# Expert layer of a two-layer diffusion step: fixed experts' weights requested first, ring slots handed out by which is left first, the next layer's weights held behind the read-back, and six output sums begun ahead of the last down product

## The chip, the cores and the metric

One core of one Trainium2 chip. The metric is device time in microseconds (us) of one execution. Engines are called as the profile calls them: PE (TensorE, matrix products), DVE (VectorE), ACT (ScalarE), POOL (GpSimd) and SP (SyncE, which here issues weight transfers). "DMA" is a transfer between device memory (DRAM) and the on-chip memory.

## The reference, cut to what matters

Two layers (`DEPTH = 2`) run over 384 tokens (128 context, 256 latent) of width 1024. The first half of a layer is attention, convolution and an output projection. The second half is a mixture of experts, and the change lies there:

```python
aff = sigmoid(t @ w_router)                  # 16 experts in 4 groups of 4
g_idx = argmax(sum of the best two of each group)
e_idx = the best two experts in that group   # top 2 per token
gates = their affinities, normalised to sum 1
hid = silu(t @ w_gate[e]) * (t @ w_up[e])    # 1024 -> 512
y = sum over the 2 experts of gates * (hid @ w_down[e])   # 512 -> 1024
x = x + gate2 * y
```

## The kernel before

All weights pass through a ring of 1 MB slots: six in `ring`, and in the expert part of a layer eight more in `extra_ring`, whose memory the rest of the layer uses. SP issues the loads in one fixed list, `RING_ORDER`. Ahead of each load it waits until the slot's earlier content has been used (`left`). It issues in order, so a load that must wait holds back all behind it.

An expert has six loads (`PER_EXPERT`): 0 and 1 are its gate matrix, 2 and 3 its up matrix, 4 and 5 its down matrix. The 16 experts form 11 units (`UNITS`): six of one expert (128 rows) and five of two experts with 64 rows each. Places 0 and 1 always hold experts 0 and 1 (`FIXED = 2`), so their loads need no routing result. Which expert stands in places 2 to 15 is decided by how crowded it is; SP reads that from `order_i` after DVE has set `order_known`. PE takes the units one after another: gate product of unit u+1, transposed hidden rows of u, up product of u+1, turned token rows of u+2, then `down(u, 0)` and `down(u, 1)`, the two halves of the down product of u. `STREAM` lists the loads in that order of use.

The outputs of units 0 to 8 are scattered by POOL to `y_rows` in DRAM and, when the last scatter has landed, read back in three transfers of 1 MB, one for each tile of 128 tokens, into `parts[0]`, `parts[1]` (both in `late`) and `parts[2]` (in `y`). ACT scales a part (`scale_part`, L1839 as called from there), DVE weighs it and adds the second half (`weigh_part`, L2552). The outputs of the last two units (9 and 10) stay on the chip: ACT and DVE split them into `y_split` (`y_high` L1848, `y_rest` L2560). For each tile t and half q of the columns a sum "A" is then collected in a PSUM bank: `add_most` is one product of the identity with the weighed part (L1420) and two products with unit 9's rows (L1430); `add_rows(t, q, LAST - 1)` adds two products with unit 10's rows. DVE multiplies each finished sum by the layer's gate and adds it to `x` (`add_last`, L2650 and L2653). In the first layer the next layer's norm follows on the same engine, in the second the output stores.

Both DVE and ACT run their lists in order. On DVE the end of a layer reads: `y_rest` of unit 9, `weigh_part` of tiles 0, 1, 2, `y_rest` of unit 10, then the sums.

Of the kernel before, what the change touches and what calls it, by code (L numbers as in the profile page):

```python
# [117 lines left out]
STREAM += unit_stream(NU - 1, 4, 6)  # L118
UNIT_OF = {k: u for u in range(NU) for k in UNITS[u]}
# [4 lines left out]
def ring_order():  # L124

    order = [(n, 2 * k + i) for n, k in FIRST_PAIRS for i in range(2)]
    for n in range(DEPTH):
        for i, js in enumerate(STAGES):
            order += [(n, S_IN + j) for j in js]
            order += [(m, 2 * k + h) for m, k in pairs_after(n, "proj", i) for h in range(2)]  # L130
            if i == S_UP_AFTER:
                order.append((n, S_UP))
        order += [(m, 2 * k + i) for m, k in pairs_after(n, "heads") for i in range(2)]
        order.append((n, S_UP + 1))
        for g in range(len(GROUPS) + 2):
            order += [(m, 2 * k + i) for m, k in pairs_after(n, "turn", g) for i in range(2)]
        order += [(n, S_OUT + j) for j in range(OUT_SLOTS)]
        order += [(n, S_EXP + e * PER_EXPERT + i) for e, i in STREAM]
# [194 lines left out]
def slots_by_turn():  # L333

    at, taken, base = [], [0] * (RING + EXTRA), 0
    before = []
    last = [None] * (RING + EXTRA)
    j = 0
    for q, (n, s) in enumerate(RING_ORDER):
        if s < S_EXP:  # L340
            r, base, j = base % RING, base + 1, 0
        else:
            if j == 0:
                cycle = [(base + i) % RING for i in range(RING)] + [RING + i for i in range(EXTRA)]
            r, j = cycle[j % len(cycle)], j + 1
# [4 lines left out]
        if s >= S_EXP and j == NE * PER_EXPERT:  # L350
            base = cycle[0]
# [14 lines left out]
def build(nc, wring, x_in, vec, rows, ckv_cache, kr_cache, nak_cache, nav_cache, cond, w_router,  # L366
          b_router, rope, shape_consts, na_bias, row_ids, no_token,
          y_prompt, y_sample, new_ckv, new_krope, new_nak, new_nav, h_rows, y_rows, tables, mod_dram):
    with ExitStack() as ctx:
# [332 lines left out]
        def _(sp):  # L702
            sp.dma_start(condT, cond).then_inc(cond_loaded, 16)
            q, expert = 0, {}
            for n in range(DEPTH):
                l = Layer(n)

# [246 lines left out]
        def _(pe):  # L954
# [180 lines left out]
            for n in range(DEPTH):  # L1135
# [300 lines left out]
                list_rows(0)  # L1436
                gate_or_up(0, "G", 0, sems["gate_half"])
# [3 lines left out]
                for u in range(NU):  # L1441
# [13 lines left out]
                    if u == NU - 2:  # L1455
                        turn_hidden(NU - 1)
                        for i in range(LAST):
                            turn_hot(i)
                    down(u, 1)

                with pe.If(extra > 0):
# [4 lines left out]
                    for i in range(LAST):  # L1466
                        pe.wait_ge(*once_read(l, (f"turned{i}",)))
                    with pe.Fori(0, extra) as w:
                        with pe.Fori(0, NE) as e:
# [25 lines left out]
                            pe.wait_ge(more_y_made[n], w * NE + (e + 1))  # L1495

                halves = [(t, q) for t in range(TILES) for q in range(2)]

                for t, q in halves[:3]:
                    add_most(t, q)  # L1500
                for t, q in halves[:3]:
                    add_rows(t, q, LAST - 1)
                for t, q in halves[3:]:
                    add_most(t, q)
# [1282 lines left out]
```

## Time and profile before

| what | value |
|---|---|
| median of 3 runs | 1071.9 us (1068.68 to 1073.7) |
| the profiled execution's own time | 1071.57 us |
| its span, first to last instruction | 1069.8 us |
| PE busy | 1006.7 us, 94% of the span |
| mean granted clock of PE | 0.97 of full |
| expert part of the first layer | from about 294 to 558 us |
| expert part of the second layer | from about 786 to 1052 us |

Times in the rows are microseconds from the start of the span. A timeline row gives start, duration, engine, source line, operation, output and inputs and the count of instructions merged in it; in brackets the idle time ahead of it and what ended it. One matrix product stands as two instructions in the trace. PEclk is the clock that PE was granted, 1.00 being 2.4 GHz and 0.50 being 1.2 GHz.

### The profile page before, as it was taken

How to read it: one execution, taken by the hardware profiler on the slowest of the kernel's cores; microseconds unless marked ns; L12 is line 12 of the kernel's file. 1: busy time of each engine (PE TensorE's matmuls, PEld its weight loads, DVE VectorE, ACT ScalarE, POOL GpSimd, SP SyncE). 2: the span in 40 equal slices, each digit the busy share in tenths (PEclk: the TensorE clock that was granted, in tenths of full speed). 3: DMA queues.
4: the chain of work that ended last, by engine and by line, in shares of the span. 5: the costliest groups of instructions: out<-in, count | busy, mean ns of one | idle time of the engine just before them, and what ended most of it. 6: DMA issues, size and time to landing. Idle time of an engine off the chain costs nothing.

```text
span 1069.8 us, 12824 instructions
## 1 busy us (share of the span) xinstructions
PE 1006.7 (94%) x4770; PEld 593.0 (55%) x4770; DVE 418.2 (39%) x861; ACT 290.9 (27%) x629; POOL 143.7 (13%) x192
## 2 busy tenths in 40 slices
PE   5899898999999999999979999889999999999975
PEld 1686556678854434444338976668874444343422
DVE  1348824586451010000136679767462100101014
ACT  2333265572111011010035337754210111101110
POOL 2200411201110000100101015201020110001000
PEclk9899989999899999999999999978999999999998
DMA  9778396864899999999981225104499999999971
GB/s 376 292 277 342 137 360 274 337 254 195 312 368 362 421 392 422 421 420 422 420 349 57 106 79 163 43 9 197 161 383 391 377 399 423 421 420 422 421 300 59
DMA packets 51376, 320.52 MB, mean 300 GB/s; under 512 B 8718, under 2 KB 8830, under 8 KB 16368
## 3 DMA queue, kind: packets, MB, share of 16 engines
q1 hardware_dynamic: 38448, 276.59, 63.9%
q0 software_dynamic: 12864, 43.08, 10.6%
q8 instruction: 40, 0.66, 0.2%
q14 instruction: 24, 0.20, 0.0%
HBM read 307.08 MB, written 21.25 MB: 307 GB/s over the span
## 4 chain that ended last, share of the span: by engine, by line
PE 76%; DVE 9%; DMA 8%; ACT 3%; issue 2%; POOL 1%; SPq 0%; DVEq 0%; POOLq 0%; ACTq 0%
PE bank L1372 26%; PE bank L1399 12%; PE bank L978 6%; PE bank L1249 5%; PE bank L996 4%; PE bank L961 3%; PE bank L1108 3%; DMA extra_ring<-wring_dram 3%; DMA y<-y_rows 2%; PE bank L1073 2%; PE bank L1039 2%; DMA ring<-wring_dram 2%; PE bank L968 2%; PE bank L1356 2%; PE bank L1285 1%
## 5 line engine op out<-in xcount | busy, mean ns | idle before, releaser
L1372 PE MATMUL bank<-ring,hgT 128*64 128x512 f32 (+1 forms) x512 | 156.4, 594 | 2.1 <-DMA ring<-wring_dram 1.6
L1372 PE MATMUL bank<-extra_ring,hgT 128*64 128x512 f32 (+1 forms) x512 | 155.9, 594 | 0.0
L1399 PE MATMUL bank<-extra_ring,hidT 128*64 128x512 f32 (+1 forms) x352 | 111.8, 624 | 9.7 <-DMA extra_ring<-wring_dram 9.7
L2533 DVE TENSOR_TENSOR sg<-bank,sg 128x512 f32<-128x512 f32 x22 | 15.2, 691 | 252.2 <-PE bank L1372 252.2
L1372 PEld LDWEIGHTS bank<-ring,hgT 128*64 128x64 f32 (+1 forms) x512 | 58.5, 157 | 87.5 <-issue 87.5
L1372 PEld LDWEIGHTS bank<-extra_ring,hgT 128*64 128x64 f32 (+1 forms) x512 | 58.3, 157 | 86.6 <-issue 86.5
L1399 PEld LDWEIGHTS bank<-extra_ring,hidT 128*64 128x64 f32 (+1 forms) x352 | 40.9, 163 | 71.4 <-issue 71.4
L2278 DVE SCALAR_TENSOR_TENSOR conv_acc<-conv_in,vecs,conv_acc 128x399 f32<-128x399 f32 x120 | 70.9, 632 | 2.1
L1108 PE MATMUL bank<-ring,cond_p 128*32 128x512 f32 x384 | 53.3, 675 | 17.0 <-DMA ring<-wring_dram 16.2
L978 PE MATMUL bank<-ring,hT 128*128 128x256 f32 x288 | 66.5, 392 | 2.6 <-DVE hT L1924 2.6
L889 POOL DMA_INDIRECT y_rows<-y,y_at x18 | 18.2, 1011 | 368.2 <-DVE y L2542 348.0
L762 POOL TENSOR_TENSOR rstd<-ms,half 128x28 f32<-128x28 f32 (+3 forms) x10 | 32.7, 3272 | 231.2 <-DVE ms L1900 231.2
L978 PEld LDWEIGHTS bank<-ring,hT 128*128 128x128 f32 x288 | 56.2, 197 | 11.6 <-DVE hT L1924 2.8
L1788 ACT COPY hgT<-bank 128x512 f32<-128x512 f32 x24 | 14.0, 585 | 167.3 <-PE bank L1356 140.4
L2542 DVE COPY y<-bank 128x512 f32<-128x512 f32 x18 | 12.4, 692 | 113.4 <-PE bank L1399 113.4
L1797 ACT ACTIVATE sg<-bank 128x512 f32<-128x512 f32 x22 | 13.1, 597 | 153.0 <-PE bank L1372 153.0
L1399 PE MATMUL bank<-ring,hidT 128*64 128x512 f32 (+1 forms) x160 | 49.6, 595 | 0.0
L1039 PE MATMUL bank<-kT,qT 96*128 96x128 f32 (+3 forms) x144 | 44.1, 441 | 0.2 <-ACT probsT L1648 0.2
L2018 DVE TENSOR_REDUCE rowmax<-bank 128x1 f32<-128x384 f32 (+1 forms) x56 | 24.8, 442 | 49.6 <-PE bank L1039 48.0
L1811 ACT COPY y<-bank 128x512 f32<-128x512 f32 x18 | 10.5, 585 | 107.6 <-PE bank L1399 107.6
L1249 PE MATMUL bank<-out_hi,mixT_hi 128*128 128x512 f32 x96 | 38.8, 404 | 1.1 <-DVE mixT_lo L2346 0.7
L1640 ACT ACTIVATE probs<-bank,negmax,qscale 128x384 f32<-128x384 f32 (+1 forms) x48 | 28.2, 594 | 34.9 <-DVE negmax L2021 34.8
(315 smaller groups left out, 1532.7 us busy)
## 6 DMA issues: line engine op xcount, KB each, us to landing
ring<-wring_dram SPq DMA_DIRECT2D x150, 1024.0 KB, 12.8
extra_ring<-wring_dram SPq DMA_DIRECT2D x108, 1024.0 KB, 17.8
y_rows<-hg POOLq DMA_DIRECT2D x6, 1024.0 KB, 6.2
kT<-mod_dram POOLq DMA_DIRECT2D x4, 1024.0 KB, 9.8
late<-y_rows POOLq DMA_DIRECT2D x4, 1024.0 KB, 15.5
ring<-wring_dram SPq DMA_DIRECT2D x4, 832.0 KB, 19.5
h_rows<-h_tok POOLq DMA_DIRECT2D x6, 512.0 KB, 6.2
ring<-wring_dram SPq DMA_DIRECT2D x4, 640.0 KB, 11.1
```

The costliest lines, as they stand in the source:

```text
L762: pool.tensor_tensor(rstd[:, 0:n], ms[:, 0:n], half[:].broadcast_to([P, n]), ALU.pow) \
L961: mm = pe.transpose(b[0:d, i * P:(i + 1) * P], part, iden[:])
L978: mm = pe.matmul(b[:, 0:n], hT[:, c, t * P:(t + 1) * P], w[:, c, :], start=(c == 0), stop=(c == KC - 1))
L996: mm = pe.matmul(b[:, 0:n], a, w, start=((c, k) == (0, 0)), stop=((c, k) == (KC - 1, 2)))
L1039: mm = pe.matmul(b[:, 0:hi - lo], qT[0:d, s, h, t * P:(t + 1) * P], kT[0:d, s, h, lo:hi], start=True, stop=True)
L1108: mm = pe.matmul(bank[b][32 * i:32 * (i + 1), :], cond_p[:, s % 2 * 4 + i, at:at + 32], w[:, i, :], start=first, stop=last)
L1249: mm = pe.matmul(b[:, :], a, w, start=((c, k) == (0, 0)), stop=((c, k) == (KC - 1, 2)))
L1372: mm = pe.matmul(b[lo:hi, :], hgT[:, 4 * i + c, lo:hi], in_ring(l, expert_slot(place, s + i))[:, c * 512:(c + 1) * 512], start=((i, c) == ...
L1399: mm = pe.matmul(b[m][lo:hi, :], hidT[:, u % 2, 2 * i + c, lo:hi], in_ring(l, expert_slot(place, 4 + i))[:, at:at + 512], start=((i, c) == ...
L1640: act.activation(out, b[:, 0:hi - lo], ACT.Exp, bias=negmax[:, g, t:t + 1], scale=qscale[:, p, 4 * t + h:4 * t + h + 1] if p < 2 else 1.0, ...
L2018: dve.tensor_reduce(rowmax[:, t:t + 1], b[:, 0:n], AX, ALU.max).then_inc(sems["dve_step"], 1)
L2278: ins = dve.scalar_tensor_tensor(conv_acc[:, c, :], conv_in[:, c, k:k + C_OUT], tap, conv_acc[:, c, :], ALU.mult, ALU.add)
```

## The change

Four edits.

1. `LOADS` replaces `STREAM` as the list in which expert weights are requested: all twelve loads of places 0 and 1 come first, then the others in the order of use as before. Two loads, the down matrix of place 1, so move ahead of the first load that needs `order_known`.
2. `slots_by_turn` no longer hands out slots in a fixed cycle. It takes the slot whose content is used up first (`left_at`).
3. At the start of the second layer's loads SP waits until all three parts of the first layer's read-back have landed (`parts_loaded`).
4. `add_most` for all six sums stands between `down(10, 0)` and `down(10, 1)`; after the last down product only the six `add_rows` for unit 10 are left. (In the branch for overfull experts, which isn't taken with these inputs, the sums are closed and begun again.)

```diff
@@ plan of the loads
+LOADS = [(k, i) for k in range(FIXED) for i in range(PER_EXPERT)] + [(k, i) for k, i in STREAM if k >= FIXED]
+USED_AT = {ki: a for a, ki in enumerate(STREAM)}
...
-        order += [(n, S_EXP + e * PER_EXPERT + i) for e, i in STREAM]
+        order += [(n, S_EXP + e * PER_EXPERT + i) for e, i in LOADS]
@@ slots_by_turn
-            if j == 0:
+            if left_at is None:
                 cycle = [(base + i) % RING for i in range(RING)] + [RING + i for i in range(EXTRA)]
-            r, j = cycle[j % len(cycle)], j + 1
+                left_at = {r: i - len(cycle) for i, r in enumerate(cycle)}
+            r = min(left_at, key=left_at.get)
+            left_at[r] = USED_AT[divmod(s - S_EXP, PER_EXPERT)]
...
-        if s >= S_EXP and j == NE * PER_EXPERT:
-            base = cycle[0]
+        if s >= S_EXP and (q + 1 == len(RING_ORDER) or RING_ORDER[q + 1][0] != n):
+            base = min(range(RING), key=left_at.get)
@@ SP, at the head of a layer
+                if n:
+                    for t in range(TILES):
+                        sp.wait_ge(parts_loaded[t], 16 * n)
@@ PE, the loop over units
+                    if u == NU - 1:
+                        for t, q in halves:
+                            add_most(t, q)
                     down(u, 1)
...
-                for t, q in halves[:3]:
-                    add_most(t, q)
-                for t, q in halves[:3]:
-                    add_rows(t, q, LAST - 1)
-                for t, q in halves[3:]:
-                    add_most(t, q)
+                for t, q in halves:
                     add_rows(t, q, LAST - 1)
```

The order of SP's instructions where the first layer's expert loads begin, in the kernel before. `bank_full...`, `x_mid`, `h_added` and `h_made` are the events that free the eight extra slots; L723 reads a routing result, L725 is a load that needs one, L719 a load that needs none.

```order
L719 DMA extra_ring<-wring_dram 128x2048 [waits bank_full3] x4
L723 TENSOR_LOAD order_i [waits order_known,bank_full4]
L723 ISA x2
L725 ISA
L725 DMA extra_ring<-wring_dram 128x2048
L723 TENSOR_LOAD order_i [waits order_known,x_mid,bank_full6]
L723 ISA x2
L725 ISA
L725 DMA extra_ring<-wring_dram 128x2048
L725 ISA [waits h_added,h_made]
```

The same place in the changed kernel (its L729, L733 and L735 are the L719, L723 and L725 of before):

```order
L729 DMA extra_ring<-wring_dram 128x2048 [waits bank_full3] x4
L729 DMA extra_ring<-wring_dram 128x2048 [waits bank_full4]
L729 DMA extra_ring<-wring_dram 128x2048 [waits x_mid,bank_full6]
L733 TENSOR_LOAD order_i [waits order_known,h_added,h_made]
L733 ISA x2
L735 ISA
L735 DMA extra_ring<-wring_dram 128x2048
L733 TENSOR_LOAD order_i [waits order_known,h_made]
L733 ISA x2
L735 ISA
L735 DMA extra_ring<-wring_dram 128x2048
L735 ISA [waits gate_half]
```

Six loads instead of four stand ahead of the wait for the routing result, and behind it two slots instead of four are free without a wait for PE. From the twenty-first expert load of a layer (the first load of place 4) on, each load stands at the same place in the list and waits for the same earlier expert load to be used up as before; only the slot's number differs.

SP's first loads of the second layer, before and then in the changed kernel:

```order
L719 DMA ring<-wring_dram 128x2048 [waits bank_full0] x2
L719 DMA ring<-wring_dram 128x1664 [waits up_half] x2
L719 DMA ring<-wring_dram 128x2048 [waits bank_full1]
L719 DMA ring<-wring_dram 128x1280 [waits bank_full1]
L719 DMA ring<-wring_dram 128x2048 [waits bank_full0]
```

```order
L729 DMA ring<-wring_dram 128x2048 [waits parts_loaded2,gate_half,parts_loaded1,parts_loaded0]
L729 DMA ring<-wring_dram 128x2048 [waits gate_half]
L729 DMA ring<-wring_dram 128x1664 [waits bank_full0] x2
L729 DMA ring<-wring_dram 128x2048 [waits down_half]
L729 DMA ring<-wring_dram 128x1280 [waits down_half]
```

The first of these six loads gains the three waits for the read-back, and all behind it stand behind that.

PE's instructions at the end of the first layer, before, from the first sum on. Ahead of them stand both halves of unit 10's down product (L1399) and the branch that isn't taken:

```order
L1420 MATMUL bank<-late,shapes 128x512
L1430 MATMUL bank<-y_split_81,turned_hot_70 128x512 x2
L1420 MATMUL bank<-late,shapes 128x512
L1430 MATMUL bank<-y_split_81,turned_hot_70 128x512 x2
L1420 MATMUL bank<-late,shapes 128x512
L1430 MATMUL bank<-y_split_81,turned_hot_70 128x512 x2
L1430 MATMUL bank<-y_split_83,turned_hot_89 128x512 x6
L1420 MATMUL bank<-late,shapes 128x512
L1430 MATMUL bank<-y_split_81,turned_hot_70 128x512 x2
L1430 MATMUL bank<-y_split_83,turned_hot_89 128x512 x2
```

In the changed kernel (L1409, L1430 and L1440 are the L1399, L1420 and L1430 of before), from inside the six sums to the last half of the down product, L1409; the first half and the first identity product stand just ahead:

```order
L1440 MATMUL bank<-y_split_81,turned_hot_70 128x512 x2
L1430 MATMUL bank<-late,shapes 128x512
L1440 MATMUL bank<-y_split_81,turned_hot_70 128x512 x2
L1430 MATMUL bank<-late,shapes 128x512
L1440 MATMUL bank<-y_split_81,turned_hot_70 128x512 x2
L1430 MATMUL bank<-late,shapes 128x512
L1440 MATMUL bank<-y_split_81,turned_hot_70 128x512 x2
L1430 MATMUL bank<-y,shapes 128x512
L1440 MATMUL bank<-y_split_81,turned_hot_70 128x512 x2
L1430 MATMUL bank<-y,shapes 128x512
L1440 MATMUL bank<-y_split_81,turned_hot_70 128x512 x2
L1409 MATMUL bank<-extra_ring,hidT 64x512 x8
```

The last half of the down product has moved behind the sums that read `y`, the third part of the read-back.

## Rows read from the trace of the kernel before

**Rows 1.** Head of the page: span, busy time of PE.

```profile
span 1069.8 us, 12824 instructions
PE 1006.7 (94%) x4770; PEld 593.0 (55%) x4770; DVE 418.2 (39%) x861; ACT 290.9 (27%) x629; POOL 143.7 (13%) x192
```

**Rows 2.** Waits of PE: us in total, times, longest.

```profile
PE bank L1399 <- DMA extra_ring<-wring_dram: 9.7, 4, 4.1
```

**Rows 3.** The chain that ended last, end of the first layer: start, us, what.

```profile
528.23 25.87 DMA y<-y_rows
...
557.40 0.72 PE bank L1430 x2
...
558.26 0.70 DVE gated_sum L2650
...
570.08 3.69 PE bank L978 x16
```

**Rows 4.** Timeline, end of the first layer.

```profile
523.42 11.45 SPq L719 DMA_DIRECT2D ring<-wring_dram  x6
...
539.94 3.65 PE L1399 MATMUL bank<-extra_ring,hidT 128*64 128x512 f32 x16 [1.06 <-DMA extra_ring<-wring_dram]
...
546.38 1.15 ACT L1839 ACTIVATE late<-late,gate 128x1024 f32<-128x1024 f32 x1 [5.74 <-DMA late<-y_rows]
547.56 1.28 DVE L2552 SCALAR_TENSOR_TENSOR late<-late,gate 128x1024 f32<-128x1024 f32 x1 [5.60 <-ACT late L1839]
...
547.64 5.11 PE L1399 MATMUL bank<-extra_ring,hidT 128*64 128x512 f32 x16 [4.05 <-DMA extra_ring<-wring_dram]
```

**Rows 5.** Timeline, end of the second layer.

```profile
1034.77 5.35 PE L1399 MATMUL bank<-extra_ring,hidT 128*64 128x512 f32 x16 [2.30 <-DMA extra_ring<-wring_dram]
...
1042.38 5.21 PE L1399 MATMUL bank<-extra_ring,hidT 128*64 128x512 f32 x16 [2.25 <-DMA extra_ring<-wring_dram]
...
1043.20 1.15 ACT L1839 ACTIVATE y<-y,gate 128x1024 f32<-128x1024 f32 x1 [3.59 <-DMA y<-y_rows]
...
1044.38 1.28 DVE L2552 SCALAR_TENSOR_TENSOR y<-y,gate 128x1024 f32<-128x1024 f32 x1 [3.45 <-ACT y L1839]
...
1047.55 1.55 DVE L2560 SCALAR_TENSOR_TENSOR y_split<-bank,gate_slot,y_split 128x512 fp32r<-128x512 f32 x2 [1.89 <-ACT y_split L1848]
...
1048.94 1.02 PE L1420 MATMUL bank<-late,shapes 128*128 128x512 f32 x2
...
1050.26 1.02 PE L1420 MATMUL bank<-late,shapes 128*128 128x512 f32 x2
...
1052.25 0.69 DVE L2650 TENSOR_TENSOR gated_sum<-bank,kT 128x512 f32<-128x512 f32 x1 [3.15 <-PE bank L1430]
```

**Rows 6.** The chain that ended last, end of the second layer.

```profile
1009.04 33.20 DMA extra_ring<-wring_dram
```

**Rows 7.** Stretches: us, busy of engines, PEclk, DMA share, GB/s.

```profile
295.00:300.00 5.00, 5.00 (x47) 4.74 (x46) 4.72 (x14) 1.24 (x3) 0.00 (x0) 1.00 0.53 187
...
335.00:340.00 5.00, 5.00 (x18) 1.89 (x18) 0.69 (x1) 0.58 (x1) 0.24 (x1) 1.00 0.80 254
...
530.00:535.00 5.00, 5.00 (x20) 2.21 (x17) 0.69 (x1) 0.00 (x0) 0.00 (x0) 1.00 1.01 416
```

**Rows 8.** Expert loads issued 334 to 340 us, from issue to landing.

```profile
DMA to landing us min/median/max: 4.7/4.8/5.0
```

**Rows 9.** The same, 826 to 832 us, second layer.

```profile
DMA to landing us min/median/max: 4.9/5.2/5.5
```

**Rows 10.** Expert loads issued 996 to 1012 us, from issue to landing.

```profile
DMA to landing us min/median/max: 25.9/27.7/33.2
```

**Rows 11.** Waits of SP: us in total, times, longest.

```profile
SPq L722 <- DVE order_i L2172: 29.6, 2, 15.1
```

**Rows 12.** DMA queues from 530 to 556 us (q1 SP's, q0 POOL's).

```profile
q1 hardware_dynamic: 1089, 7.35, 67.9%
q0 software_dynamic: 816, 3.15, 30.4%
```

**Rows 13.** Stretches at the end of the second layer: us, PE busy, PEclk, DMA, GB/s.

```profile
1036.00:1038.00 2.00, 2.00 (x8) 0.50 0.43 178
1040.00:1042.00 2.00, 0.12 (x2) 1.00 0.12 51
```

More of the change, by code:

```diff
@@ L337, in slots_by_turn @@
     last = [None] * (RING + EXTRA)
-    j = 0
+    left_at = None
     for q, (n, s) in enumerate(RING_ORDER):
         if s < S_EXP:
-            r, base, j = base % RING, base + 1, 0
+            r, base, left_at = base % RING, base + 1, None
         else:
-            if j == 0:
+            if left_at is None:
                 cycle = [(base + i) % RING for i in range(RING)] + [RING + i for i in range(EXTRA)]
-            r, j = cycle[j % len(cycle)], j + 1
+                left_at = {r: i - len(cycle) for i, r in enumerate(cycle)}
+            r = min(left_at, key=left_at.get)
+            left_at[r] = USED_AT[divmod(s - S_EXP, PER_EXPERT)]
         at.append((r, taken[r]))
@@ L1436, in _ @@
                 list_rows(0)
+                halves = [(t, q) for t in range(TILES) for q in range(2)]
                 gate_or_up(0, "G", 0, sems["gate_half"])
@@ L1467, in _ @@
                         pe.wait_ge(*once_read(l, (f"turned{i}",)))
+                    for t, q in halves:
+                        pe.matmul(bank[bank_no(l, (f"A{t}{q}",))][:, :], iden[:], parts[t][:, 0, 512 * q:512 * (q + 1)], start=False, stop=True)
                     with pe.Fori(0, extra) as w:
@@ L1495, in _ @@
                             pe.wait_ge(more_y_made[n], w * NE + (e + 1))
-                halves = [(t, q) for t in range(TILES) for q in range(2)]
-                for t, q in halves[:3]:
-                    add_most(t, q)
-                for t, q in halves[:3]:
-                    add_rows(t, q, LAST - 1)
-                for t, q in halves[3:]:
-                    add_most(t, q)
+                    for t, q in halves:
+                        add_most(t, q)
+                for t, q in halves:
                     add_rows(t, q, LAST - 1)
```

## The prediction

> **What bounds the kernel now.** I began with the page's head: PE is busy for 1006.7 of 1069.8 us [rows 1], so time is won or lost only where PE waits, runs at a lower clock, or has nothing left but a chain on other engines. The list of PE's waits comes next. Its largest in the expert part is the down product's: four waits on loads, 9.7 us in all [rows 2], two at the end of each layer. The chain that ended last and the timeline show what surrounds them. In the first layer the two halves of unit 10's down product start at 539.94 and 547.64, the second after 4.05 us of waiting and at a reduced pace, 5.11 us instead of 3.65 [rows 4]. Then the chain leaves PE: it runs through the third part of the read-back (`parts[2]`, tile 2's, "part 3" from here on), which lands at 528.23 + 25.87 = 554.10, and DVE takes up the first finished sum at 558.26; layer 2's first projection follows at 570.08 [rows 3]. In the second layer the halves start at 1034.77 and 1042.38, with waits of 2.30 and 2.25 us, and DVE starts on the sums at 1052.25 [rows 5]. There the chain goes back through the last expert load, 33.20 us from issue to landing [rows 6]. From DVE's first sum on, both ends run at DVE's pace in the kernel before and after, so **the start of DVE's first sum is the number to predict in each layer**.
>
> The stretches tell what the transfers do. Around 295 to 300 us, ahead of the routing result, they run at 187 GB/s; at 335 to 340 again only at 254; at 530 to 535 at 416 with every DMA engine busy [rows 7]. So they are late at the end and idle at the start of an expert part.
>
> **Loads of the fixed experts first, and the slots: 0 us.** SP waits for `order_i` twice, at most 15.1 us [rows 11]; two loads more, 2 MB, now go out ahead of it. At 416 GB/s a load of 1 MB takes 2.5 us, so the two fill 5.0 us of the gap; that is the most this edit could give in one layer. I take nothing, because of what comes behind. The loads issued between 334 and 340 us, the 23rd and 24th of the layer, land 4.7 to 5.0 us after issue [rows 8], in the second layer 4.9 to 5.5 [rows 9]; those issued at the end take 25.9 to 33.2 [rows 10]. A load that lands in 4.7 us has no queue ahead of it: at that moment the transfers wait for PE to free a slot. From the 21st load on each load waits for the same content to be used up as before. So whatever is gained ahead is handed back there, and the queue that makes the last loads late is built up only afterwards. The work that hides the edit is PE's own products up to there. Slots "by which is left first" only keep, for the new list, the order of use that the old cycle gave the old list. A loss from loads that now come later (the second gate loads of places 2 and 3, about 4 us) I exclude: at 335 to 340 the transfers have caught up and PE is busy throughout [rows 7].
>
> **Holding back the next layer's weights: part 3 lands about 5 us earlier, but only in the first layer.** Before, SP issues six loads for layer 2 at 523.42 to 534.87 [rows 4], behind the last expert loads, and from about 547.5 they share the DMA engines with part 3. The second layer, which has no such loads, shows part 3 without them: it lands at 1043.20 [rows 5], 0.96 us after the last expert load (1009.04 + 33.20 = 1042.24 [rows 6]). Put at the first layer's last load, 547.5, that gives 548.5; part 2's landing at 546.38 [rows 4] is the lower bound, since the parts follow one another, and 554.10, no gain, the upper one. I take 549. Parts 1 and 2 don't move; they landed while the expert loads were still in front. The loads held back start at about 549 too. With 4.7 us to land for the first [rows 8], it is there at 554 and all six by 554 + 5 x 2.5 = 566.5, ahead of the 570.08 at which the first is read [rows 3]: 16 us of cover for that one, so 0 us. If part 3 were as late as before, 11 us would remain.
>
> One rule bears on this. From 530 to 556 us SP's queue moved 1089 packets and 7.35 MB, POOL's 816 packets and 3.15 MB [rows 12]. The Trainium skill (DMA: Bandwidth & Descriptors, Queues, rings and completion order) says that each DMA engine takes turns between its queues packet by packet. By that rule the two queues are level in packets and POOL's, with the smaller ones, gets less than half of the bytes; the trace agrees. Had the turns been level in bytes, the three parts would have been in by about 528.2 + 6 x 2.5 = 543, and holding back would give nothing; the trace has 554.10, and the sum goes by that.
>
> **The six sums ahead of the last half of the down product: a gain behind it, a larger loss ahead of it.** From one `add_most` to the next are 1050.26 - 1048.94 = 1.32 us [rows 5], so the six take 7.9 us, 2.64 us for a tile. Behind the last half DVE today waits until 1052.25, that is 1052.25 - (1042.38 + 5.21) = 4.66 us. With the sums begun ahead, what remains is `y_rest` and one `add_rows`: the first half of DVE's pair at 1047.55 ends 0.7 us later at 1048.25, two instructions on PE take 0.72 [rows 3] with 0.14 of hand-over on either side, together 1.66 us behind the end of the product. That gains 3.0 us. But PE executes in order, and the last half now stands behind the two sums that read part 3. Part 3 must land, be scaled (1.15) and weighed (1.28): 1043.20 to 1045.66 [rows 5]. Behind that come 0.14, two sums of 2.64, the product of 3.65 and the 1.66, which makes 8.1 us.
>
> *Second layer.* The first half ends at 1040.12. Tile 0 runs to 1042.9, tile 1 to 1045.5, tile 2 from 1045.8 (weighed at 1045.66) to 1048.45; the last half then takes 3.65, because PE no longer stops for 2.25 us ahead of it, and ends at 1052.1; DVE starts at 1053.75 instead of 1052.25: **+1.5 us**. Were part 3 there at once, PE alone would give 1040.12 + 0.14 + 7.92 + 3.65 + 1.66 = 1053.5, +1.25: the lower bound. If the clock still falls once, as it did, 1.56 more: +3.1.
>
> *First layer.* The first half ends at 543.6, tile 0's sums at 546.4. Part 2 is weighed at 547.56 + 1.28 = 548.84 [rows 4], so PE waits 2.6 us, which it doesn't do there before. Both waits of 2.3 us in the second layer were followed by about 3.4 us at the lower of the two clocks (0.50 in 1036 to 1038 [rows 13]) and cost 1.70 and 1.56 (5.35 and 5.21 for a product of 3.65 [rows 4, 5]); I charge 1.6. Tile 1 is then done at 553.2, tile 2 (part 3 weighed at 551.5) at 555.9, the product at 559.5, and DVE starts at 561.2 instead of 558.26: **+2.9 us**. Without the fall of the clock, and part 3 in time, 551.6, 554.3, 557.9, 559.6: +1.3. With part 3 as late as 554.10 the end would be 554.10 + 2.46 + 8.1 = 564.7: +6.4; this value is far from the rows of the second layer, and I leave it out of the range. PE also has nothing to do for some 2.7 us ahead of layer 2's first transposes, where the moved sums filled the time; if the clock falls there too, up to 1.7. I take 0, since ACT and DVE set the pace there.
>
> Sum: 0 + 2.9 + 1.5 = 4.4 us on the profiled 1071.57, which lies 0.3 below the median: **1076.0 us**, 0.4% slower. About 0.5%, 5.4 us, is what a measurement of this kernel can tell from no change, so the likeliest verdict is "same".
>
> **Rivals.**
> - *The clock falls at more places* (layer 2's start 1.7, the second layer's last half 1.6): 1076.0 + 3.3 = 1079.3, slower by 0.7%. For it: both waits in [rows 5] had a fall behind them. Against it: PE's new gap in the second layer is 0.2 us. The Trainium skill (TensorE: Matmul & The Clock Gate, The HAM clock gate) says that the low clock is the resting state and that only activity releases it; by that rule this rival holds wherever the moved sums leave PE without work.
> - *The lead of the loads lasts to the end: faster.* Place: the queue at the 23rd load. If the 5.0 us survived there, loads and parts would land 5 us earlier at both ends. The second layer's DVE start would be 1043.20 - 5.0 + 2.46 + 8.1 = 1048.75, -3.5; the first's, bound by PE without waits, about 543.6 - 1.06 + 0.14 + 7.92 + 3.65 + 1.66 = 555.9, -2.4; together -5.9: 1065.7. It decides for "faster" only if nearly all of the 5.0 us survive; the 4.7 us of [rows 8] and 4.9 of [rows 9] speak against that.
> - *The sums cost less than they seem and the change is worth nothing*: no fall of the clock, part 3 in by 548. That is +1.3 + 1.25 = 2.6, 1074.2; with the runs' own scatter it reads as no change.
>
> **How the numbers follow.** Forecast and its neighbourhood (1075 to 1077.3) 0.40; no fall of the clock (1071 to 1075) 0.25; more falls, or part 3 later (above 1077.3) 0.29; lead survives 0.06. The range for 8 in 10 reaches from 1071.5 (the third rival less the 0.25% by which the runs scatter) to 1079.5 (the first rival). Slower by over 0.5% gets the 0.29, faster the 0.06, within 0.5% the remaining 0.65.
>
> **What would show it.** Loads: SP's `order_i` wait remains, loads around 335 us again land in about 4.8 us, and PE reaches 539.9 and 1034.8 (plus the first layer's shift) as before. Holding back: layer 2's six loads are issued at about 549, part 3 lands there too, and no PE wait for `ring` appears at layer 2's first projection. Sums: a PE wait of about 2.6 us for `part_weighed` between the halves in the first layer, with PEclk 0.50 behind it; the last half starts at about 556 and, counted from the same point, 6 us later than before in the second layer; DVE's first sums at about 561 and 1053.75 + 2.9 = 1056.7. I am wrong if the 23rd load's latency is no measure of the queue, if part 3 lands several us ahead of 549, or if the last half doesn't wait for it.

## The result

The changed kernel takes 1079.85 us (median of 20 runs, 1074.2 to 1091.0), the kernel before 1073.05 beside it: ratio **1.0067, 95% interval 1.0041 to 1.0094**, some 7 us slower. The forecast was 1076.0 with 1079.5 as its upper end; the time fell just beyond it, where the first rival (the clock falls at more places, 1079.3) had put it.

The span of the profiled execution is 1081.9 us, that of a second one, shown further down as e11, 1069.7. Single spans are no measure here, so the stages are read from points inside them. The page's span, which was 1069.8 before [rows 1], then PE's waits against [rows 2]:

```profile
span 1081.9 us, 12826 instructions
```

```profile
PE bank L971 <- DVE xn L1927: 5.2, 2, 2.6
PE bank L1409 <- DMA ring<-wring_dram: 3.2, 2, 2.3
...
PE bank L1430 <- DVE y L2564: 2.3, 2, 1.9
PE bank L1430 <- DVE late L2564: 2.2, 1, 2.2
```

The 9.7 us of waits for loads have become 3.2; the 4.05-us wait ahead of the last half [rows 4] is gone. In their place stand waits for the weighed parts (L1430) and, at layer 2's start, for the norm (L971). Lines are 10 higher than before on PE: L1409 is the down product, L1430 the identity product and L1440 the products with a unit's rows. The timeline of the first layer's end, to be held against [rows 4]:

```profile
542.31 3.65 PE L1409 MATMUL bank<-ring,hidT 128*64 128x512 f32 x16 [0.87 <-DMA ring<-wring_dram]
...
550.97 1.10 PE L1430 MATMUL bank<-late,shapes 128*128 128x512 f32 x2 [2.17 <-DVE late L2564]
...
551.61 1.15 ACT L1851 ACTIVATE y<-y,gate 128x1024 f32<-128x1024 f32 x1 [2.10 <-DMA y<-y_rows]
551.74 3.42 SPq L729 DMA_DIRECT2D ring<-wring_dram  x6
...
554.22 1.10 PE L1430 MATMUL bank<-y,shapes 128*128 128x512 f32 x2 [0.37 <-DVE y L2564]
...
557.03 3.65 PE L1409 MATMUL bank<-extra_ring,hidT 128*64 128x512 f32 x16
...
562.55 0.69 DVE L2662 TENSOR_TENSOR gated_sum<-bank,kT 128x512 f32<-128x512 f32 x1 [0.27 <-DVE a L2235]
...
569.29 1.09 PE L971 MATMUL bank<-shapes,xn 128*128 128x128 f32 x8 [2.59 <-DVE xn L1927]
572.97 1.97 PE L971 MATMUL bank<-shapes,xn 128*128 128x128 f32 x8 [2.59 <-DVE xn L1927]
574.73 5.09 PE L988 MATMUL bank<-ring,hT 128*128 128x256 f32 x16
```

As foretold, PE waits for part 2 (2.17 us), the held-back loads go out when part 3 is there (551.74), the last half runs at full pace and DVE's first sum follows it closely. The wait of 0.37 us for part 3 was not foretold, nor was what follows: layer 2's first projection takes 5.09 us, behind two gaps of 2.59 us on PE. The kernel before had one gap of 1.44 us there and the full pace:

```profile
568.68 1.09 PE L961 MATMUL bank<-shapes,xn 128*128 128x128 f32 x8 [1.44 <-DVE xn L1915]
570.08 3.69 PE L978 MATMUL bank<-ring,hT 128*128 128x256 f32 x16 [0.31 <-DVE hT L1924]
```

The same view at the second layer's end, against [rows 5]:

```profile
1043.66 3.65 PE L1409 MATMUL bank<-ring,hidT 128*64 128x512 f32 x16 [2.31 <-DMA ring<-wring_dram]
...
1052.09 1.15 ACT L1851 ACTIVATE y<-y,gate 128x1024 f32<-128x1024 f32 x1 [4.08 <-DMA y<-y_rows]
...
1054.70 1.19 PE L1430 MATMUL bank<-y,shapes 128*128 128x512 f32 x2 [1.90 <-DVE y L2564]
...
1056.54 1.91 PE L1430 MATMUL bank<-y,shapes 128*128 128x512 f32 x2
...
1059.15 3.65 PE L1409 MATMUL bank<-extra_ring,hidT 128*64 128x512 f32 x16
...
1064.41 0.69 DVE L2662 TENSOR_TENSOR gated_sum<-bank,kT 128x512 f32<-128x512 f32 x1
```

PE waits 1.90 us for part 3, and an identity product of 1.02 us takes 1.91. The granted clock (the number ahead of the DMA share and the GB/s) in four stretches, with PE's busy time behind the length:

```profile
551.00:553.00 2.00, 2.00 (x7) 1.18 (x7) 0.21 (x1) 1.15 (x1) 0.00 (x0) 1.00 0.23 41
...
571.00:574.00 3.00, 1.03 (x5) 1.03 (x6) 2.93 (x7) 2.15 (x8) 0.43 (x1) 0.50 0.00 0
...
1053.00:1055.00 2.00, 0.30 (x1) 0.30 (x2) 1.28 (x1) 0.24 (x1) 0.00 (x0) 1.00 0.00 0
1056.00:1058.00 2.00, 2.00 (x5) 1.03 (x4) 0.00 (x0) 0.00 (x0) 0.00 (x0) 0.50 0.00 0
```

So the clock fell at layer 2's start and behind part 3 in the second layer, not behind the wait for part 2.

**Where the 7 us are.** From the first half of the last down product to DVE's first sum, split at the last half; starts and durations are those of the rows:

| | first half to last half | last half | its end to DVE's first sum | together |
|---|---|---|---|---|
| first layer before | 7.70 | 5.11 | 5.51 | 18.32 |
| first layer after | 14.72 | 3.65 | 1.87 | 20.24 |
| second layer before | 7.61 | 5.21 | 4.66 | 17.48 |
| second layer after | 15.49 | 3.65 | 1.61 | 20.75 |

The two layers' ends are +1.9 and +3.3. From DVE's first sum to the end of the first 16 projection products it was 570.08 + 3.69 - 558.26 = 15.51 [rows 3] and is 574.73 + 5.09 - 562.55 = 17.27: +1.8. Together 7.0, as timed. That they agree so closely is in part luck: from layer 2's 17th projection product to its last down product PE's work is the same in all the kernels below, and it took from 457.8 us (e11) to 468.8 (e4) in single executions. The stages leave that out.

### The profile page after: what moved, and what is told of

It is laid out like the page before. It is cut to its first block, busy times and chain, and to the rows that moved or that the text cites. A ratio compares the mean times of both kernels' runs of the same rounds, so it can differ in the third digit from the quotient of the medians.

```text
span 1081.9 us, 12826 instructions
## 1 busy us (share of the span) xinstructions
PE 1012.1 (94%) x4770; PEld 600.0 (55%) x4770; DVE 418.1 (39%) x861; ACT 291.8 (27%) x629; POOL 143.7 (13%) x192
## 3 DMA queue, kind: packets, MB, share of 16 engines
q0 software_dynamic: 12864, 43.08, 10.5%
## 4 chain that ended last, share of the span: by engine, by line
PE 77%; DVE 8%; DMA 8%; ACT 3%; issue 2%; POOL 1%; SPq 0%; DVEq 0%; POOLq 0%; ACTq 0%
PE bank L1382 26%; PE bank L1409 12%; PE bank L988 6%; PE bank L1259 6%; PE bank L1006 4%; PE bank L971 4%; DMA y<-y_rows 4%; PE bank L1118 3%; PE bank L1083 2%; PE bank L1049 2%; DMA ring<-wring_dram 2%; PE bank L978 2%; PE bank L1366 2%; DMA y_rows<-y,y_at 2%; PE bank L1295 1%
## 5 line engine op out<-in xcount | busy, mean ns | idle before, releaser
L1382 PE MATMUL bank<-extra_ring,hgT 128*64 128x512 f32 (+1 forms) x576 | 177.6, 594 | 2.1 <-DMA extra_ring<-wring_dram 1.6
L1382 PE MATMUL bank<-ring,hgT 128*64 128x512 f32 (+1 forms) x448 | 135.1, 594 | 0.0
L1382 PEld LDWEIGHTS bank<-extra_ring,hgT 128*64 128x64 f32 (+1 forms) x576 | 66.9, 158 | 101.4 <-issue 101.3
L1382 PEld LDWEIGHTS bank<-ring,hgT 128*64 128x64 f32 (+1 forms) x448 | 50.0, 156 | 72.7 <-issue 72.7
L1409 PE MATMUL bank<-extra_ring,hidT 128*64 128x512 f32 (+1 forms) x288 | 86.0, 595 | 0.0
L1409 PE MATMUL bank<-ring,hidT 128*64 128x512 f32 (+1 forms) x224 | 71.3, 595 | 3.2 <-DMA ring<-wring_dram 3.2
L1409 PEld LDWEIGHTS bank<-extra_ring,hidT 128*64 128x64 f32 (+1 forms) x288 | 30.9, 155 | 46.3 <-issue 46.3
L1809 ACT ACTIVATE sg<-bank 128x512 f32<-128x512 f32 x22 | 13.1, 597 | 153.0 <-PE bank L1382 153.0
L1409 PEld LDWEIGHTS bank<-ring,hidT 128*64 128x64 f32 (+1 forms) x224 | 26.8, 160 | 40.0 <-issue 40.0
L1823 ACT COPY y<-bank 128x512 f32<-128x512 f32 x18 | 10.5, 585 | 107.6 <-PE bank L1409 107.6
## 6 DMA issues: line engine op xcount, KB each, us to landing
extra_ring<-wring_dram SPq DMA_DIRECT2D x108, 1024.0 KB, 17.7
late<-y_rows POOLq DMA_DIRECT2D x4, 1024.0 KB, 15.3
```

The lines of the kernel that those rows point to most:

```text
L1382: mm = pe.matmul(b[lo:hi, :], hgT[:, 4 * i + c, lo:hi], in_ring(l, expert_slot(place, s + i))[:, c * 512:(c + 1) * 512], start=((i, c) == ...
L1409: mm = pe.matmul(b[m][lo:hi, :], hidT[:, u % 2, 2 * i + c, lo:hi], in_ring(l, expert_slot(place, 4 + i))[:, at:at + 512], start=((i, c) == ...
```

## The experiments

Theory S: PE works in order, so sums ahead of the last half cost their own time and the wait for their part, and PE's gaps let the clock fall. Its rivals vary with the runs. In all of them A and C are the time from the first half of the last down product to DVE's first sum in the first and second layer, B that from the first layer's first sum to PE's 17th projection product of layer 2, each taken from the timeline of one profiled execution. "Stages" is the change of A + B + C against the kernel before, "timed" the ratio's excess times 1073 us. Single entries scatter: among the four kernels without sums ahead (before, e1, e5, e6) A is 17.5 to 19.4 and C 15.9 to 18.5. "Stages" and "timed" differ by up to 4.3 us.

| kernel | sums ahead | held back | A | B | C | stages | ratio (95% interval) | timed |
|---|---|---|---|---|---|---|---|---|
| before | 0 | no | 18.3 | 16.2 | 17.5 | | | |
| changed | 6 | yes | 20.2 | 18.0 | 20.8 | +7.0 | 1.0067 (1.0041 to 1.0094) | +7.2 |
| e1 | 0 | yes | 17.5 | 17.9 | 17.2 | +0.6 | 1.0023 (0.9987 to 1.0059) | +2.5 |
| e2 | 6 | no | 25.2 | 17.7 | 19.5 | +10.5 | 1.0124 (1.0081 to 1.0167) | +13.3 |
| e3 | 2 | yes | 13.4 | 16.4 | 13.4 | -8.8 | 0.9955 (0.9919 to 0.9990) | -4.8 |
| e4 | 6 | yes | 20.6 | 16.2 | 20.2 | +5.0 | 1.0086 (1.0049 to 1.0122) | +9.2 |
| e5 | 0 | yes | 17.5 | 16.2 | 15.9 | -2.4 | 1.0018 (0.9988 to 1.0048) | +1.9 |
| e6 | 0 | no | 19.4 | 16.2 | 18.5 | +2.2 | 1.0006 (0.9975 to 1.0037) | +0.6 |
| e7 | 2 | yes | 13.0 | 16.4 | 13.2 | -9.4 | 0.9930 (0.9896 to 0.9964) | -7.5 |
| e8 | 4 | yes | 16.1 | 17.7 | 16.0 | -2.2 | 0.9962 (0.9933 to 0.9991) | -4.1 |
| e9 | 6 | yes | 17.2 | 18.5 | 17.0 | +0.7 | 0.9995 (0.9963 to 1.0028) | -0.5 |
| e10 | 2 | no | 17.9 | 17.7 | 13.1 | -3.3 | 0.9964 (0.9933 to 0.9996) | -3.9 |
| e11 | 6 | yes | 20.6 | 17.9 | 19.8 | +6.4 | one execution, 1071.72 us | |
| e12 | 2 | no | 15.3 | 17.4 | 14.8 | -4.5 | 0.9958 (0.9929 to 0.9988) | -4.5 |

**e1: the changed kernel with the sums behind the product again.**

```diff
-                    if u == NU - 1:
-                        for t, q in halves:
-                            add_most(t, q)
                     down(u, 1)
```

> The changed kernel with the six sums back behind the last down product (edits 1 to 3 stay). Theory S (the moved sums cost all of it: the last half of the down product waits for part 3, and the clock falls in the gaps that the move leaves): part 3 no longer stands ahead of anything, DVE's first sum in the first layer comes about 0.9 us earlier than in the kernel before, second layer as before: about 1072, -0.1%. Theory H (holding back the weights costs, at layer 2's start): it stays near 1080, +0.6%. Theory L (the loads' new order or the slots cost): it stays near 1080, +0.6%.

The median is 1075.31, between S's 1072 and the 1080 of H and L. The interval holds no change and excludes the changed kernel's 0.67%, but the two intervals overlap (up to 1.0059, from 1.0041), so this run alone does not settle how much of the loss is the sums'; e2, e3 and e9 do. B is 17.9 here too: the clock fell behind a gap of 1.53 us.

**e2: the kernel before with the sums alone**, the last two pieces of the change's diff:

```diff
+                    if u == NU - 1:
+                        for t, q in halves:
+                            add_most(t, q)
                     down(u, 1)
```

> The kernel before with the six sums ahead of the last half of the down product, nothing else. Theory S: part 3 lands in the first layer as late as before, about 9 us behind the last expert load's predecessor (554 instead of 549), so DVE's first sum there comes 6.4 us later, plus up to 1.8 of lower clock at layer 2's start; second layer +3.3 as in the changed kernel: about +10 to +12 us, +0.9 to +1.1%, slower than the changed kernel. Theories H and L: no loss, 1073.

Slower by 1.2%, as S has it. Of the first layer's end, the scaling of part 3 and PE's wait for it:

```profile
553.21 1.15 ACT L1841 ACTIVATE y<-y,gate 128x1024 f32<-128x1024 f32 x1 [6.01 <-DMA y<-y_rows]
...
555.82 2.05 PE L1420 MATMUL bank<-y,shapes 128*128 128x512 f32 x2 [4.28 <-DVE y L2554]
```

Part 3 is there 1.6 us later than in the changed kernel, although the first half started earlier (541.27 against 542.31); PE waits 4.28 us instead of 0.37, and the low clock follows (2.05 us for the two products at L1420). With six sums ahead, A is 5.0 us shorter in the changed kernel, which has the hold-back and the new order of the loads as well; e6 and e7 put the order at nothing measurable, so the 5.0 are put down to the hold-back (e10 against e7: 4.9).

**e3 and e8: two and four sums ahead.** In e3, and in e8 with 4 for 2:

```diff
-                        for t, q in halves:
+                        for t, q in halves[:2]:
                             add_most(t, q)
...
-                for t, q in halves:
+                for t, q in halves[:2]:
+                    add_rows(t, q, LAST - 1)
+                for t, q in halves[2:]:
+                    add_most(t, q)
                     add_rows(t, q, LAST - 1)
```

> The changed kernel with only the two sums of tile 0 ahead of the last half of the down product, the other four behind it. Theory S: these two wait for part 1 alone, which is weighed before the first half ends, and fill PE's wait for the last load (2.3 us in the second layer, 4.0 in the first), so no gap, no fall of the clock: second layer DVE's first sum 4 us earlier than before, first layer 5 us earlier: about 1064, -0.9%. Theory H or L (the sums are not the cause): 1076 to 1080.

> The changed kernel with tile 0's and tile 1's four sums ahead, tile 2's behind the last half. Theory S (each pair ahead costs its 2.64 us and the wait for its part): the last half starts at about 553.6 in the first layer and 1052.5 in the second, as in the changed kernel without tile 2's sums; DVE's first sum is 1.9 us earlier than in the kernel before in the first layer, 3.3 in the second; together 3.5 to 4 us later than with two ahead: ratio 0.998 to 1.000, 1071 to 1073. Rival C (only the wait for part 3 costs, and with it the lower clock; PE's time for the sums is free): as with two ahead, 0.9955, about 1069.

Both are faster than the kernel before, by some 0.4%, with intervals that end below 1. A and C grow with each pair, 13.4, 16.1, 20.2 and 13.4, 16.0, 20.8. In the stages two ahead gains what S gave; the time, 1069.09, is 5 us above S's 1064, and S's 0.9% lies just outside the interval. Four ahead is 1070.68: as S's 1071 to 1073 and C's 1069 lie so close, the times don't tell them apart, but the stages do (C had two and four alike). That two ahead is faster than four is so shown by the stages of one execution each, not by the times.

**e9: no wait for a later part.** The sums of tiles 1 and 2 are started from part 1 instead of their own part, so their results, and what the second layer works on, are of other data:

```diff
-                    pe.wait_ge(sems["part_weighed"], nth(l, "part_weighed", t + 1))
-                    pe.matmul(..., iden[:], parts[t][:, 0, 512 * q:512 * (q + 1)], start=True, stop=False)
+                    pe.wait_ge(sems["part_weighed"], nth(l, "part_weighed", 1))
+                    pe.matmul(..., iden[:], parts[0][:, 0, 512 * q:512 * (q + 1)], start=True, stop=False)
```

> The changed kernel with all six sums started from part 1 instead of each tile's own part (the second and third tile's sums are of other data), so that PE between the halves of the last down product waits for no later part. Theory S (the loss is PE's waits for parts 2 and 3 ahead of the last half and the lower clock behind them; PE's own 7.9 us for the sums are paid by the 3.0 us behind and the load waits they fill): from the start of the first half to DVE's first sum 17.0 to 17.5 us in both layers, 1.3 and 0.3 less than in the kernel before, layer 2's start still 1.7 longer: ratio 1.000, 1073 to 1074. Rival O (PE's order alone costs it, whatever the parts do): 20 us in both layers as in the changed kernel, ratio 1.006, 1080.

Theory S holds, rival O falls: A 17.2, C 17.0, ratio 0.9995. In the first layer PE runs through from half to half, 11.71 us instead of 14.72:

```profile
538.48 3.65 PE L1409 MATMUL bank<-ring,hidT 128*64 128x512 f32 x16 [1.91 <-DMA ring<-wring_dram]
...
550.19 3.65 PE L1409 MATMUL bank<-extra_ring,hidT 128*64 128x512 f32 x16
```

Layer 2's start keeps its two gaps and takes 18.5 us. The interval (up to 1.0028) lies below the changed kernel's (from 1.0041). The six sums' own time is thus about paid by what they save behind the product; the loss is the waits for parts 2 and 3 and the clock.

**e11: the changed kernel once more.**

> The changed kernel once more, for the scatter of its stages. Theory S: from the first half to DVE's first sum again 20.2 us in the first layer, 20.7 in the second if the clock falls in PE's wait for part 3 there and 19.0 to 19.5 if not; layer 2's start again 18.0; the attention part anywhere from 210 to 220. Rival V (the 1.8 us at layer 2's start and in the second layer are chance): one of the two is gone, 16.2 or 19.

Both held in part: the second layer's end, then layer 2's start.

```profile
1032.30 3.65 PE L1409 MATMUL bank<-ring,hidT 128*64 128x512 f32 x16 [1.51 <-DMA ring<-wring_dram]
...
1044.07 1.10 PE L1430 MATMUL bank<-y,shapes 128*128 128x512 f32 x2 [0.84 <-DVE y L2564]
...
1046.88 3.65 PE L1409 MATMUL bank<-extra_ring,hidT 128*64 128x512 f32 x16
...
563.33 1.09 PE L971 MATMUL bank<-shapes,xn 128*128 128x128 f32 x8 [2.60 <-DVE xn L1927]
567.01 1.97 PE L971 MATMUL bank<-shapes,xn 128*128 128x128 f32 x8 [2.59 <-DVE xn L1927]
568.77 5.01 PE L988 MATMUL bank<-ring,hT 128*128 128x256 f32 x16
```

Layer 2's start is the same, so its loss is not chance. In the second layer the last half follows tile 2's first sum after 2.81 us, not 4.45: no fall behind a wait of 0.84. That fall differs between executions. The 1071.72 us of this execution lie below all 20 of the changed kernel in the result (1074.2 to 1091.0). Against the first profile, the first layer's last down product starts 6.4 us earlier (535.95) and the stretch between B and C is 5.3 us shorter, while A + B + C differ by only 0.6.

**e4: PE kept busy.** The changed kernel with idle identity products in its gaps:

```diff
+                            if (n, t, q) == (0, 1, 0):
+                                keep_busy(l, ("A10",), 8)
+                            if (n, t, q) == (1, 2, 0):
+                                keep_busy(l, ("A20",), 7)
...
-                    keep_busy(l, ("n1", 0, 0), IDLE_FIRST)
+                    keep_busy(l, ("n1", 0, 0), IDLE_FIRST + 10)
...
+                    keep_busy(l, ("n1", 1, 0), 10)
```

> The changed kernel with idle products of the identity in PE's gaps: 8 ahead of tile 1's sums in the first layer, 7 ahead of tile 2's in the second, 10 more ahead of each of layer 2's first two groups of transposes. They add no result. Theory S with the clock as half of the loss: PEclk stays 1.00 from 540 to 580 and from 1040 to 1065 us, layer 2's first projection and the second layer's last half run at full pace, 1.8 us each: about 3.5 us less than the changed kernel, 1076, +0.3%. If the waits alone make the loss and the clock doesn't matter: as the changed kernel, 1080.

A miss: 1081.92, no better than the changed kernel. Yet at layer 2's start it did what it was for:

```profile
566.20 1.09 PE L971 MATMUL bank<-shapes,xn 128*128 128x128 f32 x8 [0.38 <-DVE xn L1932]
...
569.88 1.09 PE L971 MATMUL bank<-shapes,xn 128*128 128x128 f32 x8 [0.36 <-DVE xn L1932]
571.28 3.69 PE L988 MATMUL bank<-ring,hT 128*128 128x256 f32 x16 [0.31 <-DVE hT L1941]
```

Without the gap the fall is gone, and B is 16.2: the gap causes the 1.8 us. In the second layer C changed little, for the fall came at another place. Tile 2's sums, behind the idle products, kept their pace, but this time the first half ran at the low clock, behind a wait of 2.34 us for its load (in the changed kernel it took 3.65 behind 2.31):

```profile
1044.46 5.35 PE L1410 MATMUL bank<-ring,hidT 128*64 128x512 f32 x16 [2.34 <-DMA ring<-wring_dram]
...
1056.68 1.02 PE L1431 MATMUL bank<-y,shapes 128*128 128x512 f32 x2
```

Layer 2's attention, whose instructions are the same, ran at a lower clock in this execution. The stretch from 590 to 770 us, first in the changed kernel, then in e4:

```profile
590.00:770.00 180.00, 171.42 (x888) 139.08 (x888) 131.16 (x248) 89.81 (x209) 35.18 (x37) 0.93 0.26 96
```

```profile
590.00:770.00 180.00, 174.80 (x860) 140.08 (x859) 128.08 (x246) 87.92 (x207) 35.16 (x37) 0.88 0.26 92
```

e9, without idle products, has 0.88 there too and is no slower in the timing. Whether e4's gain is always lost there, or in this execution only, stays open.

**e5 and e6: the other edits alone** on the kernel before. First the diff of e5, then of e6 (with `slots_by_turn` as in the change):

```diff
+                if n:
+                    for t in range(TILES):
+                        sp.wait_ge(parts_loaded[t], 16 * n)
```

```diff
-        order += [(n, S_EXP + e * PER_EXPERT + i) for e, i in STREAM]
+        order += [(n, S_EXP + e * PER_EXPERT + i) for e, i in LOADS]
```

> The kernel before with the hold-back alone. Theory S (the sums cause the loss, the hold-back is harmless): part 3 lands about 5 us earlier in the first layer, DVE's first sum there about 0.9 us earlier, nothing in the second layer: ratio 0.999, about 1072.5. Rival H (the 2 to 4 us that the two kernels with the hold-back lacked against the sum of their stages come from it): 1.002 to 1.004, 1075 to 1078, with layer 2's first projection later against DVE's first sum than the 16.2 us of the kernel before.

> The kernel before with the fixed experts' loads first and the slots by which is left first, nothing else. Theory S: the lead is handed back at the 23rd load, ratio 1.000, 1073. Rival L (this order costs something at the ends of the expert parts): the first half of unit 10's down product starts 1 to 2 us later in a layer, ratio 1.002 to 1.004, 1075 to 1077. Rival E (the lead lasts): down products 2 to 5 us earlier, ratio 0.995.

Neither differs from the kernel before by what this can tell. e5's time, 1075.58, would fit rival H (1075 to 1078) as well; against H speaks B, 16.2 as before, and in e6 it is 16.2 too. Two stretches of the changed kernel show the lead and how it is handed back. From 295 to 300 us the transfers run at 430 GB/s instead of 187, and they slacken (254 at 335 to 340 in [rows 7]) some 5 us sooner, at 330 to 335:

```profile
295.00:300.00 5.00, 5.00 (x47) 5.00 (x46) 4.69 (x17) 0.58 (x1) 0.00 (x0) 1.00 1.02 430
...
330.00:335.00 5.00, 5.00 (x19) 2.57 (x18) 1.39 (x2) 0.58 (x1) 0.00 (x0) 1.00 0.65 242
```

**e7, e10 and e12: what two sums ahead need.** e7 is e3 without the new order of the loads, e10 is e7 without the hold-back, and e12 is e10 with

```diff
-                for t in range(TILES):
+                for t in range(TILES - 1):
                     scale_part(t)
                 y_high(1)
+                scale_part(TILES - 1)
```

and the same on DVE (`weigh_part`, `y_rest`).

> The kernel before with the hold-back and tile 0's two sums ahead, the order of the loads as it was. Theory S (the order of the loads is worth nothing): same as the kernel that has it and two sums ahead, 0.9955, about 1069. Rival L (the order costs 2 to 4 us): 0.992 to 0.9935, 1065 to 1066.

> The kernel before with tile 0's two sums ahead of the last half and nothing else: loads and next layer's weights as before. Theory S (two sums fill PE's wait for the last load and shorten what is behind; the hold-back matters only to a sum that waits for part 3 ahead of the product): like the kernel that holds the weights back as well, ratio 0.993 to 0.996, 1067 to 1070. Rival P (part 3, landing at 554 in the first layer, holds up tile 2's sums behind the product): 2 to 3 us longer than that, ratio 0.997 to 0.999.

> The kernel before with tile 0's two sums ahead and, on ACT and DVE, the last place's y_high(1) and y_rest(1) ahead of the scaling and weighing of part 3; loads and next layer's weights as before. Theory Q (in the first layer DVE's first sum waits for part 3 only because y_rest(1) stands behind its weighing, so the hold-back buys what this order buys): from the start of the last half to DVE's first sum 5.5 us in the first layer instead of 10.2, without the hold-back; ratio 0.992 to 0.994, 1065 to 1067, like two sums ahead with the hold-back. Rival T (tile 2's sums need part 3 soon enough that nothing is won): the first sum comes earlier, but layer 2's first projection no sooner than 26 us behind the last half, ratio 0.996 to 0.998.

e7 is the fastest, 1067.04; its interval and e3's overlap, so the order of the loads is worth nothing measurable. At its first layer's end two sums fill part of PE's wait for the last load, the last half runs at full pace behind the 1.00 us that remain, and only `y_rest` and one `add_rows` remain behind:

```profile
543.54 3.65 PE L1403 MATMUL bank<-extra_ring,hidT 128*64 128x512 f32 x16 [2.07 <-DMA extra_ring<-wring_dram]
...
551.04 3.65 PE L1403 MATMUL bank<-extra_ring,hidT 128*64 128x512 f32 x16 [1.00 <-DMA extra_ring<-wring_dram]
...
556.55 0.69 DVE L2659 TENSOR_TENSOR gated_sum<-bank,kT 128x512 f32<-128x512 f32 x1 [0.27 <-DVE a L2232]
```

Against [rows 4]: 5.11 - 3.65 = 1.5 less for the product, and 556.55 - 554.69 = 1.86 instead of 5.51 behind it. Without the hold-back (e10) no sum ahead reads part 3, yet PE waits for it:

```profile
553.98 3.65 PE L1399 MATMUL bank<-extra_ring,hidT 128*64 128x512 f32 x16 [1.18 <-DMA extra_ring<-wring_dram]
...
560.91 1.28 DVE L2557 SCALAR_TENSOR_TENSOR y<-y,gate 128x1024 f32<-128x1024 f32 x1 [5.79 <-ACT y L1844]
562.11 1.41 DVE L2565 SCALAR_TENSOR_TENSOR y_split<-bank,gate_slot,y_split 128x512 fp32r<-128x512 f32 x2
...
563.00 2.04 PE L1430 MATMUL bank<-y_split,turned_hot 128*128 128x512 f32 x4 [5.37 <-DVE y_split L2565]
```

`y_rest` stands behind part 3's weighing on DVE. From the start of the last half to DVE's first sum it is 10.2 us here, 5.5 in e7. With `y_rest` first (e12) it is 7.6: theory Q's 5.5 is missed, for part 3's weighing now stands between `y_rest` and the first sum. Rival T is not borne out: the first projection follows 19.4 us behind the last half, not 26. In the second layer, where part 3 is there in time, the new order costs 1.0 us from the last half to the first sum (6.66 in e12, 5.61 in e10).

```profile
549.16 3.65 PE L1399 MATMUL bank<-extra_ring,hidT 128*64 128x512 f32 x16 [1.17 <-DMA extra_ring<-wring_dram]
...
552.78 1.55 DVE L2566 SCALAR_TENSOR_TENSOR y_split<-bank,gate_slot,y_split 128x512 fp32r<-128x512 f32 x2 [3.19 <-ACT y_split L1853]
555.12 1.28 DVE L2558 SCALAR_TENSOR_TENSOR y<-y,gate 128x1024 f32<-128x1024 f32 x1 [0.79 <-ACT y L1844]
...
556.76 0.69 DVE L2657 TENSOR_TENSOR gated_sum<-bank,kT 128x512 f32<-128x512 f32 x1 [0.27 <-DVE a L2229]
```

In e10's stages rival P holds, by more than its price, and S's "matters only to a sum that waits for part 3 ahead of the product" does not. The times don't show it: those of e7, e10 and e12 are not told apart by their intervals, e10's 0.9964 lies between what S gave (up to 0.996) and what P gave (from 0.997), the stages are from one execution each, and that of e10 lay 1% above its median (1081.17 against 1069.68).

## Why the prediction was wrong

- *Loads and slots, 0 us*: borne out within the intervals, alone (e6) and by e7 against e3.
- *Hold-back*: the part was put at 549 behind a first half at 539.94, 9.1 us later; ACT took it up at 551.61, 9.3 behind one at 542.31. The cost of 0 holds as far as can be told: no wait for `ring` appears at the projection, and e5's +1.9 us can't be told from nothing.
- *Gain behind the last half, 3.0 us*: 3.64 and 3.05.
- *First layer, +2.9*: the wait for part 2 came (2.17 for 2.6), but the 1.6 us charged for a fall of the clock there were not spent; measured +1.9, and 2.3 in the second execution, between the +2.9 and the +1.3 worked out without a fall. That term was charged too high.
- *Layer 2's start, "I take 0"*: **the step that failed.** The reason given, that ACT and DVE set the pace there, holds only up to the second transposes, which start 10.42 us behind DVE's first sum before and after (568.68 - 558.26 and 572.97 - 562.55). Behind them PE's own pace counts, and PE ran at the low clock behind two gaps of 2.59 us that the moved sums had left: +1.8 and +1.7 in two executions. e4 took the gaps away and the 1.8 with them. So the start of DVE's first sum was not the whole of what there was to predict.
- *Second layer, +1.5*: too low as well, +3.3 and +2.4. In the first execution part 3 came as early behind the product as reckoned (8.4 us), and all the excess is the clock: tile 2's sums took 1059.15 - 1054.70 = 4.45 instead of 2.64. The prediction's "new gap of 0.2 us" left out that the first half, at full clock now, ends 1.7 us sooner, which lengthens the wait to 1.90. In the second execution there was no fall; part 3 came 0.7 later behind the product.

The corrected sum is 1.9 + 1.8 + 3.3 = 7.0, or 6.4 by the second execution, for 4.4; the outcome is the one that was given 0.29. It is near the first rival's 4.4 + 3.3 = 7.7: the two falls that this rival adds came in the first execution, one of them in the second; the one charged in the first layer came in neither. The sum treated the clock as a cost of certain waits; it should have asked of every gap that the moved work leaves behind.

## What to carry to other kernels

Work moved ahead of a product on an in-order engine is free only as far as it fills a wait that is there already and reads nothing that lands later: two sums gained, six lost, and six that read nothing later (e9) cost nothing measurable. Look also at the place the work came from, since PE, left idle there, lost its clock for the stage behind. And see which short instruction stands behind a late transfer's processing on another engine; here `y_rest` did, so part 3 held up sums that don't read it.

## What the runs showed of the hardware

At layer 2's start, gaps of 2.20 to 2.61 us on PE ahead of the transposes were each followed by the lower clock (changed kernel twice, e2, e8, e9, e12), gaps of 1.45 and less never (before, e3, e4, e6, e7); of two of 1.53 one was (e1), one not (e5). e10, where the clock had fallen earlier, is left out. At other places it was less regular: 2.17 us in the first layer without a fall, 1.90 in the second with one. At the last half of the down product it went with the wait: with two sums ahead (e3, e7, e10, e12; waits of 1.18 us at most) it took 3.65 us in both layers, without sums ahead (before, e1, e5, e6; waits of 2.21 to 4.05) 5.00 to 6.26 in seven cases of eight. The Trainium skill (TensorE: Matmul & The Clock Gate, The HAM clock gate) says that the same kernel meets the gate at another phase from run to run. The second execution of the changed kernel agrees, with a span of 1069.7 us against 1081.9 and, for 590 to 770 us, this row:

```profile
590.00:770.00 180.00, 170.65 (x906) 137.16 (x906) 132.98 (x252) 89.27 (x209) 36.20 (x38) 0.96 0.29 105
```

Its attention ran at a clock of 0.96 where the first had 0.93. Differences of this size between single profiles say nothing of a change.

The two DMA queues of [rows 12] were level in packets where both had work: from 540 to 550 us SP's moved 388 packets and 2.65 MB, POOL's 388 and 1.52 MB. Over the whole stretch of [rows 12], where that was not always so, it was 1089 to 816.
